# A two-block transformer forward on one Trainium2 core: bias transfers spread over a feed-forward block, another order of VectorE's work in the first attention, other PSUM banks for the widening products, negated maxima

## The reference, cut to what matters

```python
sc = (einsum('bqhd,bshd->bhqs', qn, k_nope) + einsum('bqhd,bsd->bhqs', qr, k_rope)) * scale
p = softmax(where(causal, sc, -inf)); o = einsum('bhqs,bshd->bqhd', p, v)      # latent attention
c_kv = rmsnorm(b_ckv); k_nope, v = c_kv @ w_uk, c_kv @ w_uv; q_b = rmsnorm(b_cq) @ w_uq
s_own = einsum('bhqd,bhpd->bhqp', qb, kown) * scale + bias_own                  # second attention
```

## Time and profile before

| | us |
|---|---|
| three runs | 1010.19, 1011.52, 1012.46; median 1011.52 |
| profiled execution | 1011.16 |
| its span in the profile | 1009.3 |
| PE busy | 984.7 (98%) |
| DVE busy | 681.3 (68%) |
| ACT busy | 542.8 (54%) |
| POOL busy | 44.8 (4%) |
| mean granted TensorE clock | 0.996 of full speed |
| chain that ended last | PE 70%, issue 19%, DVE 6% |
| bytes moved | 175.89 MB, mean 174 GB/s |

### The profile page before, as it was taken

The page is one execution under the profiler, slowest core; times in us unless marked ns, Lnnn a source line. Parts: engine busy times, 40 slices in busy tenths (PEclk is TensorE's granted clock), DMA queues, the critical chain, the costliest instruction groups (busy, mean ns, idle before and its releaser), DMA issues.

```text
span 1009.3 us, 15668 instructions
## 1 busy us (share of the span) xinstructions
PE 984.7 (98%) x6348; PEld 842.5 (83%) x6348; DVE 681.3 (68%) x853; ACT 542.8 (54%) x708; POOL 44.8 (4%) x68
## 2 busy tenths in 40 slices
PE   7999999999999999999998999999999999999997
PEld 6887667898888888887887888888899898888885
DVE  5688787688777787777665555556655566555564
ACT  6676564566556565634445444444545555444452
POOL 1220000000000005000020000000000000000000
PEclk9999999999999999999999999999999999999999
DMA  9364244567565545844348656555544346556551
GB/s 307 97 207 148 87 130 146 167 205 233 177 197 188 187 161 161 262 147 155 123 139 233 207 175 206 173 203 179 180 164 166 120 158 224 189 185 199 176 165 42
DMA packets 121283, 175.89 MB, mean 174 GB/s; under 512 B 3167, under 2 KB 89770, under 8 KB 121226
## 3 DMA queue, kind: packets, MB, share of 16 engines
q1 hardware_dynamic: 118860, 168.82, 50.9%
q0 software_dynamic: 1600, 5.09, 2.0%
q10 hardware_dynamic: 766, 1.16, 0.5%
HBM read 173.82 MB, written 1.25 MB: 173 GB/s over the span
## 4 chain that ended last, share of the span: by engine, by line
PE 70%; issue 19%; DVE 6%; ACT 2%; DMA 2%; POOL 1%; SPq 0%; POOLq 0%; ACTq 0%; DVEq 0%
PE ps L1842 20%; PE ps L1892 16%; PE ps L1863 10%; PE ps L1891 7%; PE ps L1879 5%; PE ps L1906 2%; DVE w_lo L1085 1%; DMA raw<-in_ffn_w 1%; PE ps L1914 1%; PE ps L2329 1%; PE ps L1894 1%; PE ps L1957 1%; PE ps L2392 1%; PE ps L1988 1%; DMA raw<-in_w_in 1%
## 5 line engine op out<-in xcount | busy, mean ns | idle before, releaser
L1085 DVE TENSOR_TENSOR w_lo<-raw,w_hi 128x2048 fp32r<-128x2048 f32 (+3 forms) x156 | 352.3, 2262 | 129.1 <-ACT w_hi L543 128.7
L1892 PE MATMUL ps<-x_both,w_hi 128*128 128x512 f32 x992 | 342.7, 396 | 0.0
L543 ACT ACTIVATE w_hi<-raw 128x2048 fp32r<-128x2048 f32 (+3 forms) x161 | 302.3, 1879 | 63.5 <-PE ps L1842 40.1
L1891 PE MATMUL ps<-x_both,w_lo 128*128 128x256 f32 x868 | 242.0, 279 | 0.0
L1892 PEld LDWEIGHTS ps<-x_both,w_hi 128*128 128x128 f32 x992 | 179.1, 188 | 34.5
L1891 PEld LDWEIGHTS ps<-x_both,w_lo 128*128 128x128 f32 x868 | 163.6, 189 | 5.5
L798 ACT ACTIVATE work<-ps 128x512 f32<-128x512 f32 x66 | 39.3, 596 | 150.4 <-PE ps L1892 134.6
L1842 PE MATMUL ps<-w_hi,x_both 128*128 128x512 f32 (+1 forms) x320 | 101.5, 387 | 0.1
L1842 PE MATMUL ps<-w_hi,hid_hi 128*128 128x512 f32 x240 | 94.7, 394 | 3.8 <-DVE work L1489 3.3
L1842 PE MATMUL ps<-w_lo,hid_hi 128*128 128x512 f32 x240 | 93.9, 391 | 0.0
L1842 PE MATMUL ps<-w_hi,hid_lo 128*128 128x512 f32 x240 | 93.9, 391 | 0.0
(11 more groups left out here) (295 smaller groups left out, 1273.0 us busy)
## 6 DMA issues: line engine op xcount, KB each, us to landing
raw<-in_ffn_w SPq DMA_DIRECT2D x66, 1024.0 KB, 5.1
raw<-in_w_up SPq DMA_DIRECT2D x22, 1024.0 KB, 5.1
raw<-in_hgrn_w_in SPq DMA_DIRECT2D x16, 1024.0 KB, 5.5
raw<-in_w_in SPq DMA_DIRECT2D x12, 1024.0 KB, 5.1
raw<-in_moba_w_in SPq DMA_DIRECT2D x12, 1024.0 KB, 5.2
raw<-in_w_down SPq DMA_DIRECT2D x11, 1024.0 KB, 5.0
raw<-in_w_out SPq DMA_DIRECT2D x4, 1024.0 KB, 5.2
raw<-in_hgrn_w_out SPq DMA_DIRECT2D x4, 1024.0 KB, 5.0
```

The lines of the kernel that those rows point to most:

```text
L543: act.activation(w_hi[:, n % RING, 0:kc * cols], raw[:, n % RING, 0:kc * cols], ACT.Copy).then_inc(s["hi_ready"], 1)
L1085: dve.tensor_tensor(w_lo[:, n % RING, sl], raw[:, n % RING, sl], f32(w_hi[:, n % RING, sl]), ALU.subtract).then_inc(s["lo_ready"], 1)
L1891: pe.matmul(out[:, 0, :], w_lo[:, n % RING, at], x_hi[:, k, :], start=False, stop=False)
L1892: ins = pe.matmul(out, w_hi[:, n % RING, at], x_both[:, k, :, :], start=(k == 0), stop=(k == DC - 1))
```

## The change

It has six parts. (1) GpSimd's eight bias transfers each wait for a product count in the second feed-forward block: 3, 6, ... 24 granules after its start. (2) VectorE's list in the first attention: `units` calls `after(u)` between the normalising and the next maxima, and `hidden(u)` behind the maxima. The low parts of granules go to `hidden`, in halves from unit 2 on; `latent_lo` goes one unit later, into `after`; the rounds of `largest` of units 1, 2 and 4 stand in `after`; the outputs' low parts and the gating at the end are regrouped. (3) `tensor_reduce` gives the negated maxima itself; the scale that the second step held is now in the ScalarE copies of the queries. (4) Unit 6 gets its mask on TensorE. (5) The value product goes to banks 6 and 7, the query products to 2 to 5, and waits, copies and the order of low parts 10, 11 and head sums 6, 7 follow; the queries are turned by VectorE ahead of a round of `largest`. (6) `values_high` multiplies four columns by the high part, then four by the low part, each with its own wait.

```diff
@@ -65,7 +65,7 @@
...
-MASKED_BY_DVE = range(6, 16)
+MASKED_BY_DVE = range(7, 16)
...
@@ -520,6 +519,8 @@
...
             for r in range(0, P, COPIES):
+                pool.wait_ge(s["products_done"], G["ffn1"] + 3 + 3 * (r // COPIES))
                 skew = bass.AP(bias_scratch.tensor, P - 1 - r, [[HEADS * BIAS_LEN - 1, COPIES], [BIAS_LEN, HEADS], [1, S]])
...
@@ -568,13 +569,13 @@
...
-            def units(first, count, scale, psum_scores, copy_o, extra):
+            def units(first, count, psum_scores, copy_o, extra):
...
                         src, dst = psum_scores(u, j)
-                        ins = act.activation(dst, src, ACT.Exp, scale=scale(u),
+                        ins = act.activation(dst, src, ACT.Exp, scale=1.0,
                                              bias=neg_max[:, 2 * (u % 2) + j:2 * (u % 2) + j + 1],
...
@@ -644,9 +645,9 @@
...
-            def group(n, dst, src):
+            def group(n, dst, src, scale=1.0):
                 act.wait_ge(s["group_done"], n + 1)
-                act.activation(dst, src, ACT.Copy).then_inc(s["group_copied"], 1)
+                act.activation(dst, src, ACT.Copy, scale=scale).then_inc(s["group_copied"], 1)
...
@@ -704,28 +705,28 @@
...
             hi(11)
-            act.wait_ge(s["products_done"], G["uk"] + 1)
+            act.wait_ge(s["products_done"], G["uv"] + 1)
+            act.activation(v_b, ps[:, 6:8, :], ACT.Copy).then_inc(s["v_copied"], 1)
             for bank in range(2):
...
                 act.activation(kb_T[0:HD, 4 * bank:4 * bank + 3:2, :], src[0:HD], ACT.Copy)
-                act.activation(kb_T[0:HD, 4 * bank + 1:4 * bank + 4:2, :], src[HD:P], ACT.Copy)
+                ins = act.activation(kb_T[0:HD, 4 * bank + 1:4 * bank + 4:2, :], src[HD:P], ACT.Copy)
+            ins.then_inc(s["kv_copied"], 1)
...
                 act.wait_ge(s["uq_part"] if t == 0 else s["products_done"], 1 if t == 0 else G["uq"] + 1)
-                act.activation(proj[:, t, C_QB:C_QB + 768].rearrange("p (a b) -> p a b", a=2), ps[:, 6 - 2 * t:8 - 2 * t, 0:384],
+                act.activation(proj[:, t, C_QB:C_QB + 768].rearrange("p (a b) -> p a b", a=2), ps[:, 2 + 2 * t:4 + 2 * t, 0:384],
                                ACT.Copy).then_inc(s["qb_copied"], 1)
...
             copy_qb(0)
-            act.wait_ge(s["products_done"], G["uv"] + 1)
-            act.activation(v_b, ps[:, 2:4, :], ACT.Copy).then_inc(s["kv_copied"], 1)
             copy_qb(1)
...
             for j in range(4):
-                group(6 + j, qb_T[:, 2 * j:2 * j + 2, :].rearrange("p a b -> p (a b)"), ps[0:BQ, GROUP_BANKS[6 + j], :])
+                group(6 + j, qb_T[:, 2 * j:2 * j + 2, :].rearrange("p a b -> p (a b)"), ps[0:BQ, GROUP_BANKS[6 + j], :], BQ ** -0.5)
             group(10, ka_T.rearrange("p a b -> p (a b)"), ps[:, GROUP_BANKS[10], :])
             for j in range(2):
-                group(11 + j, qa_T[:, 2 * j:2 * j + 2, :].rearrange("p a b -> p (a b)"), ps[:, GROUP_BANKS[11 + j], :])
+                group(11 + j, qa_T[:, 2 * j:2 * j + 2, :].rearrange("p a b -> p (a b)"), ps[:, GROUP_BANKS[11 + j], :], HD ** -0.5)
...
@@ -1289,13 +1290,11 @@
...
                 add_heads(n)
-            lo_of(8, 9)
-            for n in range(4, 6):
-                add_heads(n)
-            lo(10)
-            for n in range(6, 8):
+            lo_of(8, 9, 10)
+            for n in range(4, 7):
                 add_heads(n)
             lo(11)
+            add_heads(7)
             then(dve.tensor_tensor(isc, isc, see, ALU.mult))
...
@@ -1317,18 +1316,18 @@
...
-            largest()
             dve.wait_ge(s["qb_copied"], 2)
...
             rotate(proj[:, :, C_QB:C_QB + 768], HEADS, BQ, HD, 16, 8, pool_tmp).then_inc(s["qb_ready"], 1)
+            largest()
             g0 = G["gate"]
...
-            ROUNDS = {0: 1, 1: 1, 3: 1, 4: 1}
-            assert 4 + sum(ROUNDS.values()) == TOPK // 8
+            ROUNDS = (0, 1, 2, 4)
+            assert 4 + len(ROUNDS) == TOPK // 8
...
@@ -1349,11 +1348,10 @@
...
                     src = prob[:, u % 2, :, :]
-                scale = 1.0 if u >= 16 else BQ ** -0.5 if u < 8 else HD ** -0.5
-                then(dve.tensor_reduce(rowmax[:, c:c + 2], src, AX_X, ALU.max))
-                dve.tensor_scalar(neg_max[:, c:c + 2], rowmax[:, c:c + 2], -scale, None, ALU.mult).then_inc(s["neg_ready"], 1)
-            def units(first, count, extra, between=None):
+                dve.tensor_reduce(neg_max[:, c:c + 2], src, AX_X, ALU.max, negate=True).then_inc(s["neg_ready"], 1)
+            def units(first, count, hidden, after):
...
@@ -1369,17 +1367,10 @@
...
                     ins.then_inc(s["prob_ready"], 1)
-                    if between:
-                        between(u)
-                    if u == 0:
-                        largest()
-                    if u == TOPK // 8 - 3:
-                        choose_keys()
+                    after(u)
                     if u + 1 < first + count:
                         maxima(u + 1)
-                    for _ in range(ROUNDS.get(u, 0)):
-                        largest()
-                    extra(u)
+                    hidden(u)
...
@@ -1426,29 +1417,43 @@
...
-            def fill_lo(u):
-                bounds(u)
-                if 1 <= u <= 8:
-                    latent_lo(u - 1)
+            ba = G["branch_a"]
+            def after1(u):
+                if 2 <= u <= 9:
+                    latent_lo(u - 2)
+                if u in ROUNDS:
+                    largest()
+                if u == 3:
+                    lo_half(g0 + 2, 1)
+                if u == 5:
+                    choose_keys()
                 if u == 14:
+                    gate_branch_b(0)
+                    output_lo1(12)
+                if u == 15:
                     dve.wait_ge(s["ohi_ready"], 1)
                     dve.tensor_tensor(x_lo[:, 0:2, :], o_T[:, 0:2, :], f32(x_hi[:, 0:2, :]), ALU.subtract).then_inc(s["olo_ready"], 1)
-                if u >= 13:
-                    output_lo1(u - 1)
-                if u in (1, 2):
-                    lo(g0 + u)
-                elif u in (5, 7, 9, 11):
-                    lo_half(g0 + 2 + u // 2, 0)
-                elif u % 2 == 1:
-                    lo(g0 + 2 + u // 2)
-                elif u in (6, 8, 10, 12):
-                    lo_half(g0 + 1 + u // 2, 1)
-                if u == 15:
-                    gate_branch_b(1)
-            units(0, 16, fill_lo, lambda u: gate_branch_b(0) if u == 14 else None)
+                    output_lo1(13)
+            def hidden1(u):
+                if u == 0:
+                    largest()
+                elif u == 1:
+                    lo(g0 + 1)
+                elif u == 2:
+                    lo_half(g0 + 2, 0)
+                elif u in (3, 4):
+                    lo_half(g0 + 3, u - 3)
+                elif u < 15:
+                    lo_half(g0 + 4 + (u - 5) // 2, (u - 5) % 2)
+                bounds(u)
+            units(0, 16, hidden1, after1)
+            output_lo1(14)
+            lo(ba + 1)
+            gate_branch_b(1)
             output_lo1(15)
-            ba = G["branch_a"]
...
@@ -2065,26 +2070,24 @@
...
             split_ready(n)
-            pe.wait_ge(s["relu_done"], 7)
+            pe.wait_ge(s["proj_copied"], 4)
             for t in range(TT):
                 for q, (x, w) in enumerate(hid_parts):
-                    ins = pe.matmul(ps[:, 2 + t, :], x[:, 2, P * t:P * t + P], w[:, n % RING, 0:512], start=(q == 0), stop=(q == 2))
+                    ins = pe.matmul(ps[:, 6 + t, :], x[:, 2, P * t:P * t + P], w[:, n % RING, 0:512], start=(q == 0), stop=(q == 2))
             ins.then_inc(s["products_done"], 1)
...
             for t in range(TT):
-                pe.wait_ge(s["proj_copied"], 4 - t)
-                if t == 1:
-                    pe.wait_ge(s["relu_done"], 8)
+                pe.wait_ge(s["relu_done"], 7 + t)
                 for half in range(2):
...
                         for q, (x, w) in enumerate(hid_parts):
-                            ins = pe.matmul(ps[:, 6 - 2 * t + half, 0:384], x[:, k, P * t:P * t + P],
+                            ins = pe.matmul(ps[:, 2 + 2 * t + half, 0:384], x[:, k, P * t:P * t + P],
                                             w[:, n % RING, 768 * k + 384 * half:768 * k + 384 * half + 384],
...
-            pe.wait_ge(s["qb_copied"], 1)
+            pe.wait_ge(s["v_copied"], 1)
             token_product(G["gate0"], 0, 6, True, False)
...
@@ -2381,14 +2384,12 @@
...
-            ready = operand_ready(6)
             def values_high(t):
...
                     pe.wait_ge(s["hi_ready"], nm + g + 1)
-                    for k in range(4):
-                        ready(t, 4 * g + k)
-                        for x in (x_hi, x_lo):
+                    for x, ready in ((x_hi, "half_hi"), (x_lo, "half_lo")):
+                        pe.wait_ge(s[ready], step(6, t, g))
+                        for k in range(4):
```

## The result

The changed kernel takes 1000.7 us (median of 4 runs, 1000.4 to 1000.92) against 1010.86 for the kernel before (4 runs, 1009.24 to 1012.46): a ratio of 0.9899, 95% interval 0.9882 to 0.9917. The forecast was 1001.9, with a range of 999.7 to 1004.8. The profiled execution took 1000.67 us with a span of 998.9, 10.4 us less than before.

The account below looks back on a forecast made before the run. TensorE, at 98% of the span, was taken as the bound, so gains come from its stops: 5.1 + 3.6 + 0.85 + 0.1 = 9.65 us off 1011.16, with 0.36 added for the median, giving 1001.9 us; range 999.7 to 1004.8.

Parts of the forecast that it names:

- rival (e): More gain than forecast: widening sums keep their 0.4 us, stages after the first attention start better; 1000.9 us, chance 0.07.
- part 4: Widening sums before the first attention: the 0.4 us stop goes but moves to the first gate product; gain 0.1 us.
- Rival (b): Second block's opening: stop only shortened, 0.8 us left with a slow restart of 1.8; 1004.5 us, chance 0.06.
- Part 1: Second feed-forward block's opening: spreading the bias transfers removes TensorE's stop and slow restart; gain 5.1 us, bounds 4.3 to 5.2.
- The slack of the steady part: Second block's steady part: weight loads have 7 us of slack, so each spread transfer's 0.8 us is hidden.
- 1.8 of slow matmuls: Second block's opening: of 5.1 us, 3.33 is standing still and about 1.8 matmuls at the lower clock after it.
- Part 2: First attention: VectorE's new order lets TensorE bound, leaving no stop; gain 3.6 us, bounds 1.8 to 3.8.
- 4.0 - 0.4: First attention: 4.0 us of TensorE idle time removed, less 0.39 for unit 6's added mask matmul; gives 3.6.
- ten stops: First attention: eight stops of 3.2 us in all behind the normalising, plus 0.5 and 0.3, all counted as gone.
- nothing of the sum hangs on: First attention: folding the negation into the reduction saves about 0.2 us per unit but leaves the forecast sum unaffected.
- Rival (a): First attention's early units bind on VectorE, margins gone, half of Part 2 stays behind; 1003.7 us, chance 0.2.
- Part 3: Second attention's border: TensorE starts on the high part after ScalarE's first copy; gain 0.85 us, bounds 0.7 to 1.1.

Follow-up runs that it names:

- bunch_later: Changed kernel, but all eight bias transfers issued at once after 12 granules of the second feed-forward block: 1001.11 us.
- all_but_bias: Changed kernel, but the eight bias transfers issued at once in the second block's opening, as before: 1003.87 us.
- order_and_step: Changed kernel with the old VectorE order in the first attention and the negation as a separate instruction again: 1005.01 us.
- high_mask5: Kernel of high_first with units 5 and 6 of the first attention masked by VectorE instead of a TensorE matmul: 999.62 us.
- old_order: Changed kernel with the old order of VectorE in the first attention, folded negation, scales and masks kept as changed: 1003.44 us.
- round_exposed: Changed kernel, but unit 0's second round of the largest stands in front of the next maxima, not under the exponentials: 1001.26 us.
- high_mask3: Kernel of high_mask5 with units 3 and 4 masked by VectorE too: 1000.43 us.
- high_first: Changed kernel with ScalarE making the first gate granule's high part between the seventh and eighth relu, not after both: 1000.27 us.
- two_step: Changed kernel with the maxima and their negation as two instructions again: 1000.79 us.

## Why the prediction was right, and where its terms were off

The forecast and its mechanism hold: the gain came out of the named stops, and no stage without idle time got some. The total is 1.2 us better than forecast. The nearest case was rival (e), 1000.9, but not for its reason: part 4 kept nothing. Rival (b) fell with the opening at 24.55 us. The terms give 0.8 of the 1.2 us (10.4 us of span against 9.65). The rest is the 0.36 that the forecast added because the median of before lay that far above its profiled run; after, the two differ by 0.03. The lower end of the range was also added up wrongly: the upper bounds of the parts make 10.55 us, so 1001.0, or 1000.3 with 0.7 for the scatter, not 1000.4 and 999.7. The result lies inside either way.

**Part 1, 5.1 us: right in size, with one reason too simple.** The opening became the third block's to the digit, and the part alone gave 5.0. The slack of the steady part hid the transfers, as predicted; bunch_later shows it even for all eight at once. By the rule of the Trainium skill that was weighed there (DMA: Bandwidth & Descriptors, anatomy of one DMA on the SWDGE path) eight would take 18.4 us one after the other, an estimate from 2.3 us each. The traces don't agree with either figure: in bunch_later the eight held the engines for about 8 us in all, and one by one beside the weight loads a transfer took 5.5 us from issue to landing (median of seven, changed kernel), and cost TensorE nothing. Wrong was to take "1.8 of slow matmuls" as a fixed piece of the stop. It stands in the one profile of before, and over 32 runs it comes and goes; all_but_bias had the stop and in its profile no slow restart. That is the likely reason why the part gave 5.0 us alone and 3.2 as the last one (5.1 was expected). It would also explain the scatter: 3.5 us over 32 runs of the kernel before, and at most 1.3 in each of the twelve kernels without the full bunch in the opening. The one of their 50 runs with a lower clock (0.996, 1006.13 us, order_and_step) has no trace, so a slow stretch may arise elsewhere too.

**Part 2, 3.6 us: 4.7 measured, above the upper bound that I gave (3.8).** Two terms were mis-sized, and one put at nothing. The step "4.0 - 0.4" took the mask matmul at its printed 0.39, but matmuls in a row overlap and it costs 0.21 to 0.23, as the two fences at high_mask5 show. And it took ten stops at their printed gaps, while each costs more. The turning of units 8 and 9, then of units 11 and 12, in the kernel before (timeline):

```profile
122.44 0.66 PE L2134 MATMUL ps<-const,work 128*128 128x128 f32 x4 [0.35 <-DVE work L1370]
127.43 0.66 PE L2134 MATMUL ps<-const,work 128*128 128x128 f32 x4 [0.34 <-DVE work L1370]
...
136.55 0.66 PE L2134 MATMUL ps<-const,work 128*128 128x128 f32 x4
141.11 0.66 PE L2134 MATMUL ps<-const,work 128*128 128x128 f32 x4
```

The stretch that ends in a gap of 0.34 takes 4.99 us (122.44 to 127.43), one without a gap 4.56 (136.55 to 141.11): the stop costs 0.43, so 0.09 more than its gap. The likely reason is that the start of a matmul then no longer overlaps the end of the one before. The same comparison, unit by unit against the changed kernel, prices the ten stops at 4.79 us for 4.00 of printed gaps, 0.06 to 0.11 more each. The mask takes 0.21 back. And 0.16 comes ahead of unit 0, where the prediction had nothing: before, the turning of the queries (L2014) starts 0.35 us after the matmul in front of it, since its weight load waits for VectorE's rotation of the queries; after, 0.23. That makes 4.79 - 0.21 + 0.16 = 4.74.

The attribution was wrong in one point: "nothing of the sum hangs on" the negation. The sum indeed hardly does, because the order alone is enough, but under the old order the negation by itself is worth 1.6 us. Each of the six stops of order_and_step is shorter by about 0.2 us in old_order, the forecast cut in each unit's chain, or gone. The mask of unit 6 was likewise priced as a cost only; under the old order two stops go with it.

**Rival (a), 0.2: did not come.** The margins were forecast at 0.3, 0.4 and 0.1 us in units 0 to 2. The trace of after shows for unit 0:

```profile
80.29 0.61 DVE L1368 TENSOR_SCALAR work<-work,stat 128x256 f32<-128x256 f32 x2
...
81.41 0.60 PE L2137 MATMUL ps<-const,work 128*128 128x128 f32 x4
```

The normalising ends at 80.9 as forecast, with 0.5 us to spare, since TensorE asks at 81.41 and not 81.26. In the next two units the same two rows give 0.8 and 0.6. But it was the wrong margin to watch: round_exposed and high_mask3 both bind first on ScalarE's copy. The rival's mechanism exists, one step further along the chain: a round of 1.7 us in front of unit 1's maxima gave a stop of 0.5, so some 1.2 us were to spare.

**Part 3, 0.85: right.** 0.72 in the profile and 0.8 by the run with the old border; TensorE starts 0.34 us after its last work instead of 1.07, on ScalarE's first copy.

**Part 4, 0.1: right in kind.** The stop moved to the first gate product, as said, behind the low part. It is 1.0 there and not the forecast 0.3 to 0.5, and the stretch came out 0.07 longer, inside the bounds. That the order of ScalarE's queue holds it was shown by high_first, which gets 0.4 back. But the prediction's reason leaves out the load: with the relu out of the way it holds the high part itself, only 0.5 us earlier.

**What the two edits together leave.** Old order and separate negation give back all of the stage but 0.55 us (94.40 against 94.95). The traces place it: 0.16 ahead of unit 0, at the turning of the queries, and 0.66 in the two stops of units 6 and 7, less 0.22 for the mask matmul, 0.60 in all. Nothing is left for the scales moved into the copies. That the mask's move took the two stops away fits their place; neither it nor the turning was run alone.

## What to carry to other kernels

Price a stop by comparing the same stretch with and without it, not by the gap printed beside it: it costs about 0.1 us more (0.06 to 0.11 here, and 0.3 at the stop of 2.8 us), and where the clock fell in it 1.8 us more in the one trace that shows it. Move a bunch of transfers to where the loads have slack; whether they are spread matters less. When two edits shorten the same chain, run each with and without the other before one of them is given the credit, and watch every queue that the chain passes through, since the first sign of too little room may stand on another engine than the one that got the work.

## What I had not expected of the hardware

- In a stop of 3.3 us TensorE's granted clock fell to 0.50 before it was over (547.6 to 547.8), and was 0.50 to 0.58 for 3.4 us of work; a stop of 2.8 us at the same place left it at 1.00. Over 32 runs the mean clock moved between 0.995 and 0.998 and the time with it, by 3.5 us.
- Eight transfers of 128 KB beside the weight loads held the DMA engines at a share of 1.0 for 8 us while the rate fell from above 310 to about 140 GB/s, although they are only 1 MB in all.
- The reduction that negates its result takes 0.69 us, as the plain one does in two_step.
